# Index weights folded into the key's panel, index scores in two batches between projection units, sums of squares folded by VectorE, and the first conv tap on ScalarE, in a two-layer fp32 kernel

## The chip, the cores and the metric

One Trainium2 chip, one of its cores. The metric is the device time of one execution in microseconds, lower is better. The profile is of one execution; its times are counted from the first instruction (the span's start).

## What is computed

A batch of one, 256 tokens of width 1024, through two layers in fp32. The change touches the first layer's front only:

```
xn = rms_norm(x, norm_g);  z = xn @ w_in          # split: q, c_kv, q_idx, k_idx, w_idx, g_attn, x_rnn, g_rnn, merge
k_idx = layer_norm(k_idx)                         # 64 wide;  c_kv = rms_norm(c_kv), 128 wide
w_idx = w_idx * 8 ** -0.5                         # 8 per token
s_idx[t, s] = sum_j relu(q_idx[t, j] . k_idx[s]) * w_idx[t, j]        # 8 index heads of 64
idx = top_k(causal(s_idx), 64)                    # the keys that attention may look at
out = conv_b + sum_k shift(x_rnn, k) * conv_w[k]  # four taps per channel
r, i = sigmoid(out @ w_a + b_a), sigmoid(out @ w_x + b_x)             # 16 blocks of 64
```

Behind it come attention over the selected keys, the recurrence, gates and output projections, and then a second layer with two attentions and 32 experts. These are the same in both kernels.

## The kernel before

**Layout.** Everything is kept transposed: channels on the 128 partitions, 256 tokens along the free dimension, so x is eight chunks of 128x256. The program is written by hand, one instruction stream per engine, with semaphores.

**Units.** The dense weights come in 140 units of 128x1024 (one output chunk of 128 channels over all eight input chunks). Two units are a panel of 1 MB, and SP loads panels into four slots of `ring`, each when PE has finished with the slot's last panel. A product is made in three passes of rounded operands: ScalarE writes the rounded high part of a unit (L989, `advance`), GpSimd subtracts it from the unit to leave the remainder in place (L1364, two instructions of 128x512 a unit), and TensorE multiplies high by high, high by remainder and remainder by high: 24 matmuls of 256 columns a unit (`chunk`, L450). The high parts have room for four units (`HI_UNITS`), so ScalarE can round unit n only when PE is done with unit n-4, and GpSimd follows ScalarE. PE needs both parts of a unit before its first matmul (`unit`). `PLAN` fixes the order of the units: 0 and 1 are `ckv_kidx`, 2 to 5 `qidx`, 6 to 13 `xrnn`, 14 to 21 `q`. Every two chunks fill one of two PSUM banks D0 and D1, which VectorE or ScalarE releases (`rel`).

**The front.** The first units are multiplied by x times the norm's gain, not yet divided by the root mean square (`x0_hi`, `x0_lo`). Meanwhile ScalarE squares x (L1008), PE sums the squares over the channels by multiplying with a matrix of ones (`sumsq`, L508, plain fp32), ScalarE takes the root (L1015), and VectorE the reciprocal (L1388). VectorE then scales what left D0 (`scaled`), makes the normalised x (`hT`, eight instructions), scales again, and makes the remainder of its rounding (`rest_of`, L1400). From `xrnn` on, units are multiplied by the normalised x. `norm` for the latent and for the index key follow on VectorE, each with a reciprocal.

**Index weights and scores.** w_idx has a small weight of its own, loaded by its own DMA (L372), split by VectorE (L1405, L1400), and multiplied on PE behind the first `xrnn` chunk: 48 matmuls of 8 columns (L543 to L547). The index key is centred by a matmul with a matrix of 1/64 (L535) and a subtraction (L1433). Then the eight heads' scores: two matmuls a head into one of two banks L0 and L1 (L555, L556, plain fp32), relu by ScalarE (L1066), product with the head's weight and sum by VectorE (L1463 to L1470, two instructions a head). A bank is used again when ScalarE has read it, and ScalarE's buffer of two when VectorE has added it. Only then PE goes on with `xrnn` 1 to 7.

**Behind them.** VectorE picks the 64 best by 16 rounds of max and replace (L1476, L1477), makes the mask (L1479, L1480), and then the convolution: four instructions a chunk, each waiting for the one before it (L1485, L1488). PE meanwhile does the eight `q` units, four products for the values (`values`, L574) and the gates' matmuls (`rg_gates`, L567): gates of chunks 0 to 3 behind q 6, of chunks 4 to 7 behind q 7. A gate waits for its chunk's convolution. The attention stage begins with scores (L595) that wait for all gates, and with VectorE instructions that wait for the mask.

## Time and profile before

| | us |
|---|---|
| median of 3 runs (757.46 to 759.19) | 758.28 |
| the profiled execution's own time | 757.45 |
| its span, first to last instruction | 755.7 |
| TensorE busy | 678.2 |
| VectorE busy | 383.3 |
| GpSimd busy | 391.3 |
| ScalarE busy | 331.7 |
| mean granted TensorE clock | 0.973 of full speed |

Busy time is the sum of an engine's instructions. An engine's busy share over the whole span averages stages with different limits; what a stage is worth is read from the order of events in it. A matmul of plain fp32 appears as two records, one of rounded operands as one.

### The profile page before, as it was taken

How to read it: one execution, taken by the hardware profiler on the slowest of the kernel's cores; microseconds unless marked ns; L12 is line 12 of the kernel's file. 1: busy time of each engine (PE TensorE's matmuls, PEld its weight loads, DVE VectorE, ACT ScalarE, POOL GpSimd, SP SyncE). 2: the span in 40 equal slices, each digit the busy share in tenths (PEclk: the TensorE clock that was granted, in tenths of full speed). 3: DMA queues.
4: the chain of work that ended last, by engine and by line, in shares of the span. 5: the costliest groups of instructions: out<-in, count | busy, mean ns of one | idle time of the engine just before them, and what ended most of it. 6: DMA issues, size and time to landing. Idle time of an engine off the chain costs nothing.

```text
span 755.7 us, 13893 instructions
## 1 busy us (share of the span) xinstructions
PE 678.2 (90%) x5634; PEld 564.6 (75%) x5634; DVE 383.3 (51%) x672; ACT 331.7 (44%) x604; POOL 391.3 (52%) x284
## 2 busy tenths in 40 slices
PE   4899999999999999989999999998899998677754
PEld 4879989888998999989789899997745453334321
DVE  3869954489998145996856556433410110010002
ACT  5534476875546346664348755441321211111102
POOL 3837855588878999979879666781000000000000
PEclk9969999999999999999999999999999999999987
DMA  8714533443434455544444334599799999999992
GB/s 326 281 57 141 186 120 112 143 137 112 165 120 163 167 175 200 171 134 160 167 167 168 116 132 144 209 421 423 304 423 419 422 421 421 422 420 422 421 419 88
DMA packets 26274, 181.73 MB, mean 240 GB/s; under 512 B 3040, under 2 KB 3296, under 8 KB 4832
## 3 DMA queue, kind: packets, MB, share of 16 engines
q1 hardware_dynamic: 26208, 180.81, 62.6%
q8 instruction: 47, 0.77, 0.4%
q14 instruction: 19, 0.16, 0.1%
HBM read 179.75 MB, written 1.05 MB: 239 GB/s over the span
## 4 chain that ended last, share of the span: by engine, by line
PE 63%; DMA 13%; DVE 11%; ACT 5%; issue 4%; POOL 2%; SPq 2%; ACTq 0%; DVEq 0%
PE D L450 36%; PE L L869 6%; DMA xT<-w_expert_dram 4%; DMA hT<-w_expert_dram 4%; DMA big<-w_expert_dram 4%; PE L L849 3%; PE QB L899 3%; POOL ring_r L1364 2%; DMA ring<-w_dense_dram 2%; PE D L490 2%; DVE big L1381 2%; PE L L595 1%; PE D L906 1%; DVE big_r L1400 1%; DVE big_r L1405 1%
## 5 line engine op out<-in xcount | busy, mean ns | idle before, releaser
L1364 POOL TENSOR_TENSOR ring_r<-ring,ring_r 128x512 fp32r<-128x512 f32 x280 | 391.1, 1431 | 120.7 <-ACT ring_r L989 120.3
L450 PE MATMUL D<-scr_r,ring_r 128*128 128x256 f32 x1104 | 214.1, 290 | 0.7 <-DVE big L1381 0.7
L989 ACT ACTIVATE ring_r<-ring 128x1024 fp32r<-128x1024 f32 x140 | 146.2, 1053 | 90.9 <-PE D L450 80.4
L450 PEld LDWEIGHTS D<-scr_r,ring_r 128*128 128x128 f32 x1104 | 176.4, 193 | 3.4 <-issue 2.1
L450 PE MATMUL D<-hT_r,ring_r 128*128 128x256 f32 x552 | 156.7, 284 | 0.0
L450 PE MATMUL D<-big_r,ring_r 128*128 128x256 f32 x1110 | 138.1, 284 | 1.6 <-POOL ring_r L1364 1.6
L450 PEld LDWEIGHTS D<-big_r,ring_r 128*128 128x128 f32 x1110 | 134.6, 192 | 3.4 <-issue 2.3
L450 PEld LDWEIGHTS D<-hT_r,ring_r 128*128 128x128 f32 x552 | 106.4, 193 | 1.2 <-issue 1.0
L1381 DVE SCALAR_TENSOR_TENSOR th<-th,L 64x256 f32<-64x256 f32 x32 | 13.4, 418 | 179.7 <-ACT th L1295 179.2
L1295 ACT ACTIVATE th<-L 64x256 f32<-64x256 f32 x16 | 6.0, 377 | 86.1 <-PE L L869 86.1
L849 PEld LDWEIGHTS L<-cst,big 128*128 128x128 f32 x256 | 29.8, 191 | 12.2 <-issue 12.2
L869 PE MATMUL L<-big,small 128*32 128x256 f32 x416 | 29.7, 394 | 8.8 <-DMA big<-w_expert_dram 7.8
L1118 ACT ACTIVATE attn<-attn,stat 128x128 f32<-128x128 f32 x64 | 28.4, 446 | 20.3 <-DVE stat L1508 20.3
L1515 DVE TENSOR_SCALAR attn<-attn,stat 128x128 f32<-128x128 f32 x64 | 34.7, 584 | 1.1
L1400 DVE TENSOR_TENSOR big_r<-big,big_r 128x256 fp32r<-128x256 f32 (+1 forms) x32 | 32.1, 1011 | 6.3 <-ACT big_r L1182 2.8
L849 PE MATMUL L<-cst,big 128*128 128x128 f32 x256 | 32.8, 281 | 1.6 <-DVE cst L1794 0.9
L1285 ACT ACTIVATE small<-L 128x512 f32<-128x512 f32 x16 | 9.6, 597 | 54.3 <-PE L L849 54.3
L869 PE MATMUL L<-ring,small 128*32 128x256 f32 x320 | 23.1, 412 | 10.6 <-DMA ring<-w_expert_dram 10.6
L1126 ACT ACTIVATE attn<-TB 128x384 f32<-128x384 f32 x32 | 15.5, 485 | 34.6 <-PE TB L604 34.6
L869 PEld LDWEIGHTS L<-big,small 128*32 128x32 f32 x416 | 15.9, 112 | 17.9 <-issue 11.4
L869 PEld LDWEIGHTS L<-ring,small 128*32 128x32 f32 x320 | 12.1, 116 | 18.5 <-issue 14.2
L1381 DVE SCALAR_TENSOR_TENSOR big<-big,D 128x512 f32<-128x512 f32 x16 | 10.9, 683 | 27.1 <-PE D L450 27.1
(335 smaller groups left out, 1032.2 us busy)
## 6 DMA issues: line engine op xcount, KB each, us to landing
ring<-w_dense_dram SPq DMA_DIRECT2D x69, 1024.0 KB, 4.9
big<-w_expert_dram SPq DMA_DIRECT2D x40, 1024.0 KB, 25.0
ring<-w_expert_dram SPq DMA_DIRECT2D x30, 1024.0 KB, 26.3
wu<-w_expert_dram SPq DMA_DIRECT2D x6, 1024.0 KB, 24.7
attn<-w_expert_dram SPq DMA_DIRECT2D x5, 1024.0 KB, 20.2
scr<-w_expert_dram SPq DMA_DIRECT2D x5, 1024.0 KB, 27.3
hT<-w_expert_dram SPq DMA_DIRECT2D x5, 1024.0 KB, 27.6
xT<-w_expert_dram SPq DMA_DIRECT2D x5, 1024.0 KB, 26.0
```

The lines of the kernel that those rows point to most:

```text
L450: last = mm(out_, r32(w[i][ws]), r32(x[j][xs_]), start=start and m == 0, stop=stop and m == 2)
L490: mm(bank[:, u * T:(u + 1) * T], r32(w[h][:, k * P:(k + 1) * P]), r32(src[0][:, k, :]), start=(u + k + h == 0), stop=False, skip_group_che ...
L849: last = mm(X[:, c * P:(c + 1) * P], htok[:, tt, (4 * half + c) * P:(4 * half + c + 1) * P], sel[:, g % 2, tt, :], start=(tt == 0), stop=( ...
L869: last = mm(G[at_:at_ + WIN, 0:FF], x(4 * h + k, e), w[e][:, m, k, :], start=(h + k == 0), stop=(h * 4 + k == DC - 1))
L899: last = mm(DN[at_:at_ + WIN, :], actT[:, b, k, e * WIN:(e + 1) * WIN], w[e][:, k, h, :], start=(k == 0), stop=(k == 1))
L989: A_(r32(hi_unit(j)), dense_unit(j), ACT.Copy).then_inc(hi_ready, 1)
L1118: last = A_(E[:, a % 2, c0:c0 + n], S[:, a % 2, c0:c0 + n], ACT.Exp, bias=stat[:, a % 2, 0, tt:tt + 1], accum_out=stat[:, a % 2, 1, tt:tt ...
L1126: A_(PT[:, a % 2, :], TB[:, 0:CAUSAL], ACT.Copy).then_inc(pt_ready, 1)
L1364: last = g.tensor_tensor(r32(w), w, r32(h).bitcast(F32), ALU.subtract)
L1381: return v.scalar_tensor_tensor(out=out_, in0=in0, scalar=scalar, in1=in1, op0=op0, op1=op1)
L1400: v.tensor_tensor(r32(f), f, r32(hi[:, per * i:per * i + per, :]).bitcast(F32), ALU.subtract).then_inc(lo_of[name], 1)
L1515: last = v.tensor_scalar(E[:, a % 2, c0:c0 + n], E[:, a % 2, c0:c0 + n], stat[:, a % 2, 2, tt:tt + 1], None, ALU.mult)
```

## The change

- The eight columns of w_idx take the place of the second copy of the index key in the panel of `ckv_kidx` (64 columns of key, 8 of weights, zeros). The 48 matmuls, their split and their DMA are gone; two matmuls of 8 columns with the identity turn the weights over (L539 of the changed kernel), and ScalarE copies them out.
- The index key is centred by one matmul with a centring matrix of 64 rows, whose result the norm reads from PSUM; the subtraction is gone. The key's norm comes ahead of the latent's.
- The scores go into four banks (L0, L1, TB, OB) in two batches of four heads, one behind `xrnn` 1 and one behind `xrnn` 2. The order of the norm, the units' rounding and the relus on ScalarE is written anew.
- VectorE adds the squares of x pairwise, three additions of 128x512, so that PE sums two chunks, not eight; that sum comes behind `ckv_kidx` 1.
- The convolution's first tap (with the bias) is two ScalarE instructions of 128x256 for each bank of `xrnn`, read from PSUM; VectorE has three instructions a chunk left.
- The softplus of the recurrence's decay and its two table loads come first on ScalarE, and a one-column square root behind unit 1 loads the root's table.
- The values' first matmuls wait for the last relu, since they use two of the four banks.

The diff, cut to its core:

```diff
...
-NORMS = [(8, D), (1, LAT), (1, 1), (8, D), (8, D), (6, QL), (2, KL), (8, D)]
-N_X, N_CKV, N_KIDX, N_FIN1, N_ATT2, N_CQ, N_CKV2, N_FFN = range(8)
+NORMS = [(8, D), (1, IDXD), (1, LAT), (8, D), (8, D), (6, QL), (2, KL), (8, D)]
+N_X, N_KIDX, N_CKV, N_FIN1, N_ATT2, N_CQ, N_CKV2, N_FFN = range(8)
...
+        IB = [L0, L1, TB, OB]
...
-            sp_.dma_start(widx_w[:], w_widx.rearrange("p (c t) -> p c t", c=DC)).then_inc(s_in["widx"], 16)
...
             first_chunk(open_bank("ckv_kidx", 0)[:, 0:T])
-            sumsq(N_X)
             chunk("ckv_kidx", 1, x0)
+            pe.wait_ge(x_folded, 1)
+            for c in range(2):
+                last = mm(UB[:, 0:T], ones, scr[:, c, :], start=(c == 0), stop=(c == 1))
+            last.then_inc(ssq, 1)
             chunk("qidx", 0, x0)
...
-            mm(OB[:, 0:T], C("mean64", P), zc[:, 1, :], start=True, stop=True).then_inc(mean_ready, 1)
+            for tt in range(NT):
+                mm(QB[:, tt * IDXH:(tt + 1) * IDXH], zc[IDXD:P, 1, tt * P:(tt + 1) * P], ident[IDXD:P, IDXD:IDXD + IDXH],
+                   start=(tt == 0), stop=(tt == NT - 1), skip_group_check=True)
+            mm(OB[:, 0:T], C("center", P)[0:IDXD], zc[0:IDXD, 1, :], start=True, stop=True).then_inc(centered, 1)
             chunk("qidx", 1, x0)
-            sumsq(N_CKV, src=sq1)
+            pe.wait_ge(rooted, N_KIDX)
+            pe.wait_ge(sq, SQ0[N_KIDX] + 1)
+            mm(UB[:, 0:T], ones[0:IDXD], sq1[0:IDXD, 1, :], start=True, stop=True).then_inc(ssq, 1)
             chunk("qidx", 2, x0)
-            sumsq(N_KIDX, C("mean64", P), src=sq1[:, 1:2, :])
             chunk("qidx", 3, x0)
+            sumsq(N_CKV, src=sq1)
             chunk("xrnn", 0, h2, split="x")
-            pe.wait_ge(lo_of["widx"], 1)
-            for tt in range(NT):
-                for k in range(DC):
-                    last = mm3(QB[:, tt * IDXH:(tt + 1) * IDXH], h2, (widx_hi, widx_w),
-                               np.s_[:, k, tt * P:(tt + 1) * P], np.s_[:, k, :], k == 0, k == DC - 1)
-            last.then_inc(widx_mm, 1)
+            chunk("xrnn", 1, h2)
+
+            def idx_scores(j0):
+
+                for j in (j0, j0 + 2):
+                    if j >= 4:
+                        pe.wait_ge(idx_relu, j - 2)
+                    for tt, (c0, n) in enumerate(((0, P), (P, T))):
+                        for i in range(2):
+                            lo = IDXD * i
+                            last = mm(IB[(j + i) % 4][:, c0:c0 + n], qi[lo:lo + IDXD, j // 2, tt * P:(tt + 1) * P],
+                                      kiT[lo:lo + IDXD, 0:n], start=True, stop=True)
+                            if tt:
+                                last.then_inc(idx_mm, 1)
...
             pe.wait_ge(kidx_ready, 1)
             kept(pe, "qidx", 1)
...
-            for c in range(1, 8):
+            idx_scores(0)
+            chunk("xrnn", 2, h2)
+            idx_scores(4)
+            for c in range(3, 8):
                 chunk("xrnn", c, h2)
...
+                pe.wait_ge(v1_ready, n - 1) if n >= 2 else pe.wait_ge(idx_relu, IDXH)
...
             squares(N_X, x_in)
+            advance(2)
+            act.wait_ge(vstep, 1)
+            A_(stat[:, 0, 2, 0:1], sp[:, 9, 0:1], ACT.Sqrt)
             advance(HI_UNITS)
             rootmean(N_X)
-            advance(HI_UNITS + 1)
+            advance(HI_UNITS + 2)
+            act.wait_ge(centered, 1)
+            A_(widx, QB[:, 0:2 * IDXH].rearrange("p (a b) -> p a b", a=2), ACT.Copy,
+               scale=float(IDXH ** -0.5)).then_inc(widx_ready, 1)
+            A_(sq1[:, 1, :], OB[:, 0:T], ACT.Square).then_inc(sq, 1)
...
-                   ACT.Copy).then_inc(rel["act"], 1)
-
-            for j in range(IDXH):
-                act.wait_ge(idx_mm, j + 1)
-                if j >= 2:
-                    act.wait_ge(idx_acc, j - 1)
-                A_(S[:, j % 2, :], LB[j % 2][:, 0:CAUSAL], ACT.Relu).then_inc(idx_relu, 1)
+                A_(xr[:, 2 * i:2 * i + 2, CONV:CONV + T], bank[:, :].rearrange("p (a b) -> p a b", a=2), ACT.Copy)
+                for m in range(2):
+                    c = 2 * i + m
+                    last = A_(u[:, c, :], bank[:, m * T:(m + 1) * T], ACT.Identity, bias=V("conv_b", c),
+                              scale=V("conv_w", 3 * 8 + c))
+                last.then_inc(rel["act"], 1)
+
+            def idx_relus(j0):
+
+                for j in range(j0, j0 + 4):
+                    act.wait_ge(idx_mm, j + 1)
+                    if j >= 4:
+                        act.wait_ge(idx_acc, j - 3)
+                    A_(scores_in[:, j % 4, :], IB[j % 4][:, 0:CAUSAL], ACT.Relu).then_inc(idx_relu, 1)
+
+            advance(UNIT0["xrnn"] + 1 + HI_UNITS)
+            idx_relus(0)
             conv_in(0)
+            advance(UNIT0["xrnn"] + 3 + HI_UNITS)
+            idx_relus(4)
...
+            dve.wait_ge(sq, 2)
+            v.tensor_tensor(scr[:, 0:2, :], scr[:, 0:2, :], scr[:, 2:4, :], ALU.add)
+            dve.wait_ge(sq, 4)
+            step(v.tensor_tensor(scr[:, 4:6, :], scr[:, 4:6, :], scr[:, 6:8, :], ALU.add))
+            v.tensor_tensor(scr[:, 0:2, :], scr[:, 0:2, :], scr[:, 4:6, :], ALU.add).then_inc(x_folded, 1)
...
+            dve.wait_ge(centered, 1)
+            norm(N_KIDX, lambda c: OB[:, 0:T], lambda c: kiT, "idx_ln_gain")
+            dve.wait_ge(normed, NM0[N_KIDX] + 1)
+            v.tensor_scalar(kiT, kiT, V("idx_ln_bias"), None, ALU.add).then_inc(kidx_ready, 1)
+            scaled("qidx", 1, qi[:, 2:4, :], float(IDXD ** -0.5))
+            dve.wait_ge(rel["dve"], 1)
+            norm(N_CKV, lambda c: zc[:, 0, :], lambda c: cT, "kv_norm_gain")
...
-                step(v.tensor_scalar(u[:, c, :], xr[:, c, 4:4 + T], V("conv_w", 3 * 8 + c), V("conv_b", c),
-                                     ALU.mult, ALU.add))
...
```

**TensorE, from the first chunk to the third `qidx` unit.** D are the projections' banks, UB holds sums of squares, OB the centred key or its mean, QB the index weights. Before:

```order
L525 MATMUL D<-big_r,ring_r 128x256 x8
L508 MATMUL UB<-scr,vec 128x256 x8
L450 MATMUL D<-big_r,ring_r 128x256 x48
L535 MATMUL OB<-small,cst 128x256
L450 MATMUL D<-big_r,ring_r 128x256 x24
L508 MATMUL UB<-small,vec 128x256
L450 MATMUL D<-big_r,ring_r 128x256 x24
L508 MATMUL UB<-small,cst 128x256
```

and in the changed kernel:

```order
L524 MATMUL D<-big_r,ring_r 128x256 x8
L449 MATMUL D<-big_r,ring_r 128x256 x24
L532 MATMUL UB<-scr,vec 128x256 x2
L449 MATMUL D<-big_r,ring_r 128x256 x24
L539 MATMUL QB<-cst,small 128x8 x2
L541 MATMUL OB<-small,cst 128x256
L449 MATMUL D<-big_r,ring_r 128x256 x24
L545 MATMUL UB<-small,vec 128x256
```

The sum over x moved behind unit 1 and shrank from eight matmuls to two, and the sum behind the first `qidx` pair is now the key's, not the latent's.

**ScalarE, from the rounding of the first units to the key's root.** `scr` is the rounded normalised x, `ring` the units, `root` a root. Before:

```order
L989 ACTIVATE ring_r<-ring 128x1024 x3
L1015 ACT_TABLE_LOAD
L1015 ACTIVATE root<-UB,sp 128x256
L989 ACTIVATE ring_r<-ring 128x1024
L1038 ACTIVATE scr_r<-hT 128x512 x2
L989 ACTIVATE ring_r<-ring 128x1024
L1038 ACTIVATE scr_r<-hT 128x512 x2
L1008 ACTIVATE small<-small 128x256
L1015 ACTIVATE root<-UB,sp 128x256
```

and in the changed kernel:

```order
L1045 ACT_TABLE_LOAD
L1045 ACTIVATE stat<-sp 128x1
L1000 ACTIVATE ring_r<-ring 128x1024 x2
L1026 ACTIVATE root<-UB,sp 128x256
L1000 ACTIVATE ring_r<-ring 128x1024 x2
L1050 ACTIVATE small<-QB 128x16
L1052 ACTIVATE small<-OB 128x256
L1057 ACTIVATE scr_r<-hT 128x512 x2
L1000 ACTIVATE ring_r<-ring 128x1024
L1057 ACTIVATE scr_r<-hT 128x512 x2
L1026 ACTIVATE root<-UB,sp 128x256
```

The table load left the path to the root, the square that PE's next sum needs stands ahead of the rounding of the normalised x and not behind it, and units 4 and 5 are both rounded before it.

**VectorE, from the normalised x to the first addition of scores.** `small` holds the index queries, the key and the latent; D and OB are PSUM. Before:

```order
L1381 SCALAR_TENSOR_TENSOR hT<-xT,vec,th 128x256 x8
L1381 SCALAR_TENSOR_TENSOR small<-D,th 128x512
L1433 TENSOR_TENSOR small<-small,OB 128x256
L1400 TENSOR_TENSOR hT_r<-hT,scr_r 128x512 x4
L1388 RECIPROCAL rinv<-root 128x256
L1381 SCALAR_TENSOR_TENSOR small<-small,vec,rinv 128x256
L1388 RECIPROCAL rinv<-root 128x256
L1381 SCALAR_TENSOR_TENSOR small<-small,vec,rinv 128x256
L1441 TENSOR_SCALAR small<-small,vec 128x256
L1381 SCALAR_TENSOR_TENSOR small<-D,th 128x512
```

and in the changed kernel:

```order
L1401 SCALAR_TENSOR_TENSOR hT<-xT,vec,th 128x256 x8
L1401 SCALAR_TENSOR_TENSOR small<-D,th 128x512
L1420 TENSOR_TENSOR hT_r<-hT,scr_r 128x512 x4
L1408 RECIPROCAL rinv<-root 128x256
L1401 SCALAR_TENSOR_TENSOR small<-OB,vec,rinv 128x256
L1475 TENSOR_SCALAR small<-small,vec 128x256
L1401 SCALAR_TENSOR_TENSOR small<-D,th 128x512
L1408 RECIPROCAL rinv<-root 128x256
L1401 SCALAR_TENSOR_TENSOR small<-small,vec,rinv 128x256
```

The key's reciprocal, product and bias now stand ahead of the latent's, the subtraction is gone, and the key is read from PSUM.

## Rows read from the trace of the kernel before

**Rows 1.** The page: the chain that ended last, by engine.

```profile
PE 63%; DMA 13%; DVE 11%; ACT 5%; issue 4%; POOL 2%; SPq 2%; ACTq 0%; DVEq 0%
```

**Rows 2.** Windows: length, busy us (count) of PE, PEld, DVE, ACT, POOL, clock, DMA.

```profile
42.40:47.70 5.30, 5.30 (x29) 5.28 (x28) 2.57 (x9) 0.21 (x1) 1.19 (x1) 0.52 0.00 0
...
60.00:78.30 18.30, 18.30 (x155) 18.30 (x154) 17.23 (x47) 7.88 (x10) 15.29 (x13) 1.00 0.52 173
```

**Rows 3.** The chain of waits in order of time: start, us, what.

```profile
3.22 0.95 SPq L372
...
20.43 0.49 ACT root L1015
...
20.94 1.77 DVE th L1388
...
30.83 2.87 PE D L450 x24
...
40.11 7.61 PE QB L450 x48
...
56.36 3.73 PE D L450 x17
...
110.90 1.97 PE L L567 x8
```

**Rows 4.** TensorE's timeline: start, us, line, tiles, count, idle before and its releaser.

```profile
15.38 3.62 PE L508 MATMUL UB<-scr,vec 128*128 128x256 f32 x16
...
30.16 0.67 PE L508 MATMUL UB<-small,vec 128*128 128x256 f32 x2 [2.11 <-ACT small L1008]
...
37.07 2.08 PE L473 MATMUL D<-scr_r,ring_r 128*128 128x256 f32 x16
...
116.09 0.93 PE L595 MATMUL L<-small,big 64*128 64x128 f32 x8
```

**Rows 5.** GpSimd's timeline: the remainders of the units.

```profile
14.48 2.50 POOL L1364 TENSOR_TENSOR ring_r<-ring,ring_r 128x512 fp32r<-128x512 f32 x2 [2.29 <-ACT ring_r L989]
18.25 7.73 POOL L1364 TENSOR_TENSOR ring_r<-ring,ring_r 128x512 fp32r<-128x512 f32 x6 [1.28 <-ACT ring_r L989]
28.75 2.97 POOL L1364 TENSOR_TENSOR ring_r<-ring,ring_r 128x512 fp32r<-128x512 f32 x2 [2.77 <-ACT ring_r L989]
```

**Rows 6.** VectorE's timeline, 23 to 56 us.

```profile
23.34 5.30 DVE L1381 SCALAR_TENSOR_TENSOR hT<-xT,vec,th 128x256 f32<-128x256 f32 x8
28.57 0.68 DVE L1381 SCALAR_TENSOR_TENSOR small<-D,th 128x512 f32<-128x512 f32 x1
29.16 0.41 DVE L1433 TENSOR_TENSOR small<-small,OB 128x256 f32<-128x256 f32 x1
29.49 5.08 DVE L1400 TENSOR_TENSOR hT_r<-hT,scr_r 128x512 fp32r<-128x512 f32 x4
34.50 1.74 DVE L1388 RECIPROCAL rinv<-root 128x256 f32<-128x256 f32 x1
36.27 0.99 DVE L1381 SCALAR_TENSOR_TENSOR small<-small,vec,rinv 128x256 f32<-128x256 f32 x1
...
39.99 1.24 DVE L1441 TENSOR_SCALAR small<-small,vec 128x256 f32<-128x256 f32 x1
...
54.32 1.60 DVE L1381 SCALAR_TENSOR_TENSOR small<-attn,small 128x128 f32<-128x128 f32 x4 [0.63 <-ACT attn L1066]
```

**Rows 7.** VectorE's timeline, 58 to 123 us.

```profile
58.17 0.29 DVE L1476 MAX8 small<-small 128x8 f32<-128x128 f32 x1
...
75.22 4.35 DVE L1381 SCALAR_TENSOR_TENSOR big<-big,vec 128x256 f32<-128x256 f32 x3
...
117.12 0.56 DVE L1381 SCALAR_TENSOR_TENSOR attn<-small,L 128x384 f32<-128x384 f32 x1 [11.13 <-PE L L595]
...
121.41 1.67 DVE L1515 TENSOR_SCALAR attn<-attn,stat 128x128 f32<-128x128 f32 x2
```

**Rows 8.** Groups by line and form, VectorE, 0 to 114 us: count, busy us, mean ns.

```profile
L1381 DVE SCALAR_TENSOR_TENSOR big<-big,vec 128x256 f32<-128x256 f32 x24 | 23.8, 992 | 0.9
```

More of the change, by code:

```diff
@@ L113 @@
 _c = 0
-for _name, _n in [("ident", P), ("mean64", P), ("swap", P), ("before", P), ("dist", CAUSAL),
+for _name, _n in [("ident", P), ("center", P), ("swap", P), ("before", P), ("dist", CAUSAL),
                   ("causal", CAUSAL), ("cos_mla", T), ("sin_mla", T), ("cos_moba", T), ("sin_moba", T),
@@ L119, with build @@
 NCST = _c
-def build(nc, x_t, vecs, consts, w_widx, w_rg, w_uk, w_uv, w_kr, w_router, w_dense, w_expert, final_row, out):
+def build(nc, x_t, vecs, consts, w_rg, w_uk, w_uv, w_kr, w_router, w_dense, w_expert, final_row, out):
     ctx = ExitStack()
@@ L206, in build @@
         sq1 = at(small, 2 * K + 512, 2, T)
+        scores_in = at(attn, 0, 4, CAUSAL)
         cqT = at(big, 0, QC, T)
@@ L277, in build @@
         vstep, astep = sem("vector_step"), sem("scalar_step")
-        mean_ready, centered, kidx_ready, widx_mm, widx_ready = [sem(n) for n in (
-            "mean_ready", "centered", "kidx_ready", "widx_matmul", "widx_ready")]
+        x_folded, centered, kidx_ready, widx_ready = [sem(n) for n in (
+            "x_squares_folded", "kidx_centered", "kidx_ready", "widx_ready")]
         idx_mm, idx_relu, idx_acc = sem("idx_scores"), sem("idx_relu"), sem("idx_accumulated")
@@ L1019, in x_in @@
                 return xT[:, c:c + w, :]
-            act.wait_ge(s_in["vec"], 16)
-            act.wait_ge(vstep, 1)
-            A_(root[:, 0:1], sp[:, 9, 0:1], ACT.Copy)
+            act.wait_ge(sp_step, 2)
+            A_(sp[:, 2, :], sp[:, 1, :], ACT.Exp, scale=-1.0).then_inc(sp_act, 1)
+            act.wait_ge(sp_step, 3)
+            A_(sp[:, 4, :], sp[:, 3, :], ACT.Ln).then_inc(sp_act, 1)
             for c in range(DC):
@@ L1408, in _ @@
             step(v.memset(sp[:, 9, :], EPS))
+            dve.wait_ge(s_in["vec"], 16)
+            v.tensor_scalar(sp[:, 0, :], V("lru_lambda", 0, 8), -1.0, None, ALU.mult).then_inc(sp_step, 1)
+            dve.wait_ge(sp_step, 1)
+            v.tensor_tensor(sp[:, 1, :], sp[:, 0, :], V("lru_lambda", 0, 8), ALU.max).then_inc(sp_step, 1)
+            dve.wait_ge(sp_act, 1)
+            v.tensor_scalar(sp[:, 3, :], sp[:, 2, :], 1.0, None, ALU.add).then_inc(sp_step, 1)
+            dve.wait_ge(sp_step, 3)
+            step(v.tensor_scalar(sp[:, 5, :], sp[:, 3, :], 1.0, None, ALU.is_equal))
+            step(stt(sp[:, 6, :], sp[:, 3, :], -1.0, sp[:, 5, :], ALU.add, ALU.add))
+            step(v.reciprocal(sp[:, 7, :], sp[:, 6, :]))
             for c in range(DC):
@@ L1415, in _ @@
             v.memset(xr[:, :, 0:CONV], 0.0).then_inc(padded, 1)
-            v.tensor_scalar(sp[:, 0, :], V("lru_lambda", 0, 8), -1.0, None, ALU.mult).then_inc(sp_step, 1)
-            dve.wait_ge(sp_step, 1)
-            v.tensor_tensor(sp[:, 1, :], sp[:, 0, :], V("lru_lambda", 0, 8), ALU.max).then_inc(sp_step, 1)
-            dve.wait_ge(s_in["widx"], 16)
-            split("widx", widx_w, widx_hi, 0, DC)
+            dve.wait_ge(sp_act, 2)
+            step(v.tensor_tensor(sp[:, 6, :], sp[:, 4, :], sp[:, 5, :], ALU.add))
+            step(v.tensor_tensor(sp[:, 6, :], sp[:, 6, :], sp[:, 2, :], ALU.mult))
+            step(v.tensor_tensor(sp[:, 6, :], sp[:, 6, :], sp[:, 7, :], ALU.mult))
+            step(stt(sp[:, 6, :], sp[:, 0, :], 0.0, sp[:, 6, :], ALU.max, ALU.add))
+            step(v.tensor_scalar(sp[:, 7, :], sp[:, 6, :], LRU_C / 2, None, ALU.mult))
+            v.tensor_scalar(sp[:, 8, :], sp[:, 6, :], -LRU_C / 2, None, ALU.mult).then_inc(sp_ready, 1)
             rinv0 = th[:, 0, 0:T]
@@ L1467, in _ @@
                     acc = score[:, c0:c0 + n]
-                    last = stt(acc, S[:, j % 2, c0:c0 + n], widx[:, tt, j:j + 1],
+                    last = stt(acc, scores_in[:, j % 4, c0:c0 + n], widx[:, tt, j:j + 1],
                                acc if j else C("causal", n, c0), ALU.mult, ALU.add)
@@ L1919, in constants @@
     c["ident"] = np.eye(P)
-    c["mean64"] = ((i[:, None] // 64) == (i[None, :] // 64)) / 64.0
+    c["center"] = np.where(i[:, None] < 64, (i[:, None] == i[None, :] % 64) - 1.0 / 64.0, 0.0)
     r = i % 64
@@ L1960, in pack @@
     uv = k_major(ukv[:, :, HD2:].reshape(KL, 512)).reshape(P, UNIT)
-    parts = [chunks_of(a) for a in (np.concatenate([ckv, ki, ki], 1), qi, xr, q, ga, gr, mg,
+    parts = [chunks_of(a) for a in (np.concatenate([ckv, ki, np.pad(wi, ((0, 0), (0, 64 - IDXH)))], 1), qi, xr, q, ga, gr, mg,
                                     g["w_rnn_proj"][0], g["w_attn_proj"][0], g["w_out"][0], cq, ck, qb, kb)]
```

57 lines of the change are left out of this document (8 added, 49 removed).

## The prediction

> **What bounds the kernel now.** I read the chain of waits by engine first: TensorE holds 63% of it [rows 1], so I look for stretches in which TensorE waits, works slowly or does work that can go. The windows and the chain in order of time show such a stretch in the first layer's front. The 48 matmuls of 8 columns for the index weights take 7.61 us from 40.11 [rows 3], and while they run the granted clock falls: it is 0.52 of full speed from 42.4 to 47.7 [rows 2], so the array is at its lower level, 1.2 GHz of 2.4. The scores behind them last until 56.36, that is 8.64 us, and the next unit still pays for the clock: 17 matmuls in 3.73 us [rows 3], where a unit of 24 takes 2.87 at full clock [rows 3]. Ahead of that TensorE waits once, 2.11 us for a square of ScalarE [rows 4]. From 60 to 78 it has no gap [rows 2], and the gates' last matmuls begin at 110.90 [rows 3]. VectorE is done with the convolution at about 106, since its first attention instruction at 117.12 follows 11.13 us of idleness [rows 7]. So up to the gates TensorE is the path, with some slack for VectorE.
>
> **The sum, followed along TensorE.** I build the times of the changed kernel from the durations of the rows and compare at fixed points.
>
> *To unit 6 (xrnn 0).* Unit 1 starts when its remainder is there, 14.48 + 2.50 = 16.98 [rows 5], and ends at 19.85. The sum over x is now two matmuls; eight took 3.62 [rows 4], 0.45 each, so it ends at 20.75. The squares were there at 15.38 at the latest, when the old sum began [rows 4]; three VectorE additions of 1.27, by the 5.08 for four of that size [rows 6], end by 19.2 and hide behind unit 1. The root takes 0.49, the reciprocal 1.77 [rows 3], the scaling 0.68 [rows 6]: 23.75. The root's table load, which stood just ahead of the root, goes to a place where ScalarE waited for a panel; but the root is no earlier (20.75 against 20.43 [rows 3]), because the sum comes later. Unit 2 has its remainder at 18.25 + 7.73/3 = 20.8 [rows 5] and fills TensorE until 23.7. The transposes and the centring take about 0.7: 24.5. Then unit 3 to 27.3, the key's sum 0.45 to 27.8 (its square is ready, since it now stands ahead of the rounding of x), units 4 and 5 to 33.55, the latent's sum to 34.0. Before, unit 6 began at 37.07 [rows 4]. **Gain 3.1.**
>
> *Index weights.* Gone with their 48 matmuls: **gain 7.6** [rows 3]. Their DMA is 32 KB; its issue, 0.95 on SP and on the chain [rows 3], is gone too, and the panels behind it may land up to that much earlier. I count nothing, since by the path above unit 1 is in place earlier and units 2 and 3 follow closely; the 0.95 goes into the low end.
>
> *Scores.* At full clock a pair of heads of the same shapes takes 0.86 to 0.93, by the attention's own pair [rows 4]. Two batches of two pairs make 3.5, in place of 8.64: **gain 5.1.** The second batch waits for the third relu of the first, which has a whole unit (2.87) to come. What stands behind a late relu on ScalarE is the rounding of units 11 to 13; TensorE comes to those only 8 to 14 us later.
>
> *Clock.* The 17 matmuls at half clock would take 17/24 of 2.87 = 2.03, so **gain 1.7.** Around 30 TensorE was idle for 2.11 and the unit behind it still took 2.87 [rows 3, 4], so I expect the short waits that are left to cost no clock.
>
> *The new wait.* The scores need the key and the second index queries, and these come at the end of a VectorE chain: from 23.75 eight normalised chunks, a scaling 0.68, four remainders 5.08, reciprocal 1.74, key, bias 1.24, scaling 0.68 [rows 6]. The key is read from PSUM now; a product of that size with one operand in PSUM took 0.41, one with both in SBUF 0.99 beside GpSimd [rows 6]. The eight chunks took 5.30 [rows 6], but GpSimd was idle for the last of them, from 25.98 to 28.75 [rows 5], because ScalarE had not rounded unit 5. In the changed order it has, and GpSimd works on. If the last four took 0.40, like small ones alone [rows 6], the first four took 0.92 each; eight of these are 7.4. That makes 41.0. TensorE is through unit 7 at 34.0 + 2 x 2.87 = 39.75. **Loss 1.2**; 0 if the eight take 5.30, 2.5 if key and reciprocals are held up as well.
>
> *Behind it.* ScalarE gets eight taps, 3.9 in all if each takes what the root of the same size took, 0.49 [rows 3], in a stage where it is busy for 7.88 of 18.3 [rows 2]; they are hidden. The five units behind the second batch, q, values and gates are as before.
>
> Sum: 3.1 + 7.6 + 5.1 + 1.7 - 1.2 = 16.3 gained. Against the profiled execution's own 757.45 that is 741.15; the median of the runs is 0.8 higher, so I give **742.0** for the median. Everything behind the gates is started by semaphores and should only move; the loads of the experts too, since the first of them waits for the attentions' last product.
>
> **VectorE, next in line.** The latent follows the key: 41.0 + 1.74 + 0.99 = 43.7, and the additions of scores start there. They took 0.40 each without GpSimd [rows 6]; now GpSimd rounds beside them, and a pair of small instructions beside it took 1.67 [rows 7]. So eight heads take 6.4 to 13.4, ending at 50 to 57. The 16 rounds and the mask took from 58.17 to about 73.8 (75.22 less the first tap, 1.4) [rows 7], 15.6: 66 to 73. The convolution's 24 remaining instructions took 23.8 [rows 8], in a mix of 0.5 alone and 1.45 beside GpSimd [rows 7]: 90 to 97. TensorE asks for the last gates' inputs from 110.9 - 16.3 = 94.6 on, two microseconds long. I count no stall, but the slack of about 5 is nearly spent.
>
> The rows show the additions only with GpSimd idle, so a page bears on them. The Trainium skill (SBUF — State Buffer, "Who interferes with whom") says that a VectorE instruction with two inputs in SBUF contends with GpSimd's reads, and one with at most one such input, outside the two-port modes, does not. That speaks against this change, which moves 16 additions with both inputs in SBUF beside GpSimd's work: by the 0.40 of the rows the forecast stands with its slack, by the rule it moves towards rival 1. The trace agrees with the rule so far, in 0.41 with an operand in PSUM against 0.99 with both in SBUF [rows 6].
>
> **Rivals.**
> 1. *The mask comes late and the convolution stops TensorE* (17%). For it: every addition and tap is slowed beside GpSimd. Against it: GpSimd gets work only as TensorE finishes units, four ahead, so a waiting TensorE soon frees VectorE. Additions 13.4, and all 24 instructions at 1.45, 34.8: 57 + 15.6 + 34.8 = 107.4, against 96: up to 11 lost, 753. A part of it, 3 to 7, is likelier: 745 to 749.
> 2. *The front is quicker* (15%): no new wait, panels 0.95 earlier. 16.3 + 1.2 + 0.95 = 18.5, so 739.8.
> 3. *The gain is given back* (3%): the attention stage or the experts' loads wait for something that did not move, and the time stays at 758. Only the first loads have no semaphore ahead of them, and by the rows above they are used long after.
> 4. *Slower* (3%): VectorE becomes the bound outright. If the 16 additions of scores take 1.45 each (23.2, by the convolution's chained ones [rows 7]), the mask is ready at 82.5 and the convolution at 117.3. The old last gates needed it by about 112, so it decides from 112 on; at 117.3 the kernel loses 5: 763. It needs GpSimd to be busy all the way, which a stopped TensorE prevents.
>
> **How the numbers follow.** The forecast's own case (741 to 744) has 62%, the rivals 17, 15, 3 and 3%. The range 738.8 to 748.0 takes in rival 2 and the likelier part of rival 1. A measurement of this kernel can tell 0.2%, 1.5 us, from no change. Faster 0.95, within it 0.02, slower 0.03.
>
> **What would show it.** In the profile after: unit 6 at about 34 and a granted clock of 1.00 from 37 to 60 (gain of the clock); two batches of scores of under 2 us each, the first after a wait of 0 to 2.5 behind the key; xrnn's last unit ending at about 61.6; VectorE's additions of scores slower than 0.40 each, the first max at 50 to 57; the gates' first matmuls without a wait for the convolution. The forecast is wrong if the clock falls again at the scores, if the first gates wait for VectorE by more than 3, or if the distance from the gates to the end is no longer the same.

## The result, and the profile after

| | before | after |
|---|---|---|
| median of four runs each, us | 758.24 (757.46 to 759.19) | 748.29 (746.90 to 749.74) |
| ratio, with its 95% interval | | 0.9850 (0.9826 to 0.9873) |
| the profiled execution's own time, us | 757.45 | 748.94 |
| its span, us | 755.7 | 747.1 |
| VectorE busy, us | 383.3 | 388.1 |

By the medians the kernel is faster by 10.0 us; the ratio with its interval says 11.4 us (9.6 to 13.2). Forecast were a gain of 16.3 and a time of 742.0, with a range to 748.0; the median lies 0.3 above the range. The page of the changed kernel, its chain by engine:

```profile
PE 56%; DVE 19%; DMA 12%; issue 4%; ACT 4%; POOL 2%; SPq 2%; ACTq 0%; DVEq 0%
```

VectorE has 19% where it had 11 [rows 1]: it has become the path for a stretch. Windows of the changed kernel (columns as in [rows 2]):

```profile
15.50:18.20 2.70, 0.03 (x1) 0.03 (x1) 2.67 (x3) 1.83 (x3) 2.62 (x2) 0.83 1.02 431
18.20:23.60 5.40, 5.40 (x25) 5.40 (x26) 5.15 (x8) 1.29 (x2) 4.98 (x4) 0.50 1.01 419
...
42.40:47.70 5.30, 5.30 (x48) 4.79 (x47) 5.19 (x7) 3.72 (x7) 5.30 (x5) 1.00 0.43 131
```

The clock at the scores is whole now (1.00 from 42.4 on, where it was 0.52), but it is at its lower level from 18.2 to 23.6, where it was 1.00 before. TensorE's timeline:

```profile
18.17 5.49 PE L449 MATMUL D<-big_r,ring_r 128*128 128x256 f32 x24 [2.80 <-POOL ring_r L1384]
23.46 1.36 PE L532 MATMUL UB<-scr,vec 128*128 128x256 f32 x4
...
38.42 2.26 PE L472 MATMUL D<-scr_r,ring_r 128*128 128x256 f32 x16
...
44.45 0.93 PE L560 MATMUL L<-small 64*128 64x128 f32 x8
...
97.90 1.10 PE L579 MATMUL L<-big 128*128 128x256 f32 x4 [0.72 <-ACT big L1099]
100.47 1.13 PE L579 MATMUL L<-big 128*128 128x256 f32 x4 [1.47 <-DVE big L1401]
...
104.83 0.93 PE L606 MATMUL L<-small,big 64*128 64x128 f32 x8
```

Ahead of unit 1 TensorE stands idle for 2.80 us behind GpSimd, and then the unit takes 5.49 us instead of 2.87 [rows 3]. Unit 6 begins at 38.42, later than in the first profile of before (37.07 [rows 4]) and not at 34.0. The wait of 2.11 that stood ahead of the latent's sum [rows 4] is gone. The scores begin without a wait. The last gates, whose second pair began at 110.90 [rows 3], begin it at 97.90, 13.0 earlier, but wait 1.47 in its middle for the convolution. The attention's scores come at 104.83 instead of 116.09 [rows 4]. VectorE's timeline:

```profile
15.23 1.77 DVE L1447 TENSOR_TENSOR scr<-scr 128x512 f32<-128x512 f32 x1
16.92 1.23 DVE L1448 TENSOR_TENSOR both_gains<-vec 128x8 f32<-128x8 f32 x1
...
22.45 1.20 DVE L1458 TENSOR_SCALAR sp<-sp 128x8 f32<-128x8 f32 x1
25.36 1.75 DVE L1408 RECIPROCAL th<-root 128x256 f32<-128x256 f32 x1 [1.71 <-ACT root L1026]
...
27.76 6.24 DVE L1401 SCALAR_TENSOR_TENSOR hT<-xT,vec,th 128x256 f32<-128x256 f32 x8
...
34.52 6.53 DVE L1420 TENSOR_TENSOR hT_r<-hT,scr_r 128x512 fp32r<-128x512 f32 x4
...
42.75 0.48 DVE L1401 SCALAR_TENSOR_TENSOR small<-OB,vec,rinv 128x256 f32<-128x256 f32 x1
43.27 0.35 DVE L1475 TENSOR_SCALAR small<-small,vec 128x256 f32<-128x256 f32 x1
...
47.46 2.80 DVE L1401 SCALAR_TENSOR_TENSOR small<-attn,small,cst 128x128 f32<-128x128 f32 x2
...
79.35 21.07 DVE L1401 SCALAR_TENSOR_TENSOR big<-big,vec 128x256 f32<-128x256 f32 x24
105.86 0.55 DVE L1401 SCALAR_TENSOR_TENSOR attn<-small,L 128x384 f32<-128x384 f32 x1 [5.45 <-PE L L606]
```

The chain of waits of the changed kernel (start, us, what) goes almost wholly by VectorE from the first reciprocal to the last tap:

```profile
27.84 6.16 DVE hT L1401 x8
...
47.46 2.81 DVE small L1401 x2
...
99.05 1.38 DVE big L1401
...
100.47 1.13 PE L L579 x4
```

The additions of scores last from 47.46 to the first max at 62.80, 15.3 us, and 5.45 us of idleness are left where there were 11.13 [rows 7].

**Three distances.** The first matmul comes when x and the first unit have landed, 9.56 to 10.55 us after the start in the thirteen profiles of this study, whatever the kernel. So I cut each profile into: from the first matmul to the start of `xrnn` 0 (*front*); from there to the attention's first scores (*middle*); from there to the end of the span (*rest*).

| profile | front | middle | rest |
|---|---|---|---|
| before | 27.51 | 79.02 | 639.6 |
| before, second profile | 28.62 | 78.99 | 642.0 |
| before with the fold alone | 28.95 | 77.44 | 641.8 |
| after | 28.14 | 66.41 | 642.3 |
| after, second profile | 26.98 | 66.42 | 642.0 |
| no fold | 24.65 | 66.83 | 642.3 |
| filler matmuls | 26.53 | 64.67 | 642.4 |
| fewer rounds | 26.99 | 64.66 | 642.5 |
| mask later | 28.08 | 64.65 | 641.6 |
| no fold and mask later | 25.88 | 64.67 | 642.2 |
| tap back | 26.97 | 69.57 | 641.6 |
| one batch | 26.40 | 68.24 | 644.1 |
| late softplus (filler, mask later) | 25.52 | 64.66 | 640.7 |

Forecast were 24.4 (34.0 less 9.56), 65.8 (79.0 less 7.6, 5.1 and 1.7, plus 1.2) and an unchanged rest. The middle came out within a microsecond, but by luck: the wait for the key that the forecast counted (1.2) did not come, and a wait for the convolution that it did not count (1.8) did. The front did not come out. The rest looks 2.7 us longer than in before's first profile, and not longer than in its second.

### The profile page after: what moved, and what is told of

It reads as the page before. It is cut to its first block, busy times and chain, and to the rows that moved or that the text cites. A ratio compares the mean times of both kernels' runs of the same rounds, so it can differ in the third digit from the quotient of the medians.

```text
span 747.1 us, 13776 instructions
## 1 busy us (share of the span) xinstructions
PE 666.2 (89%) x5578; PEld 554.3 (74%) x5578; DVE 388.1 (52%) x664; ACT 333.6 (45%) x611; POOL 392.8 (53%) x284
## 4 chain that ended last, share of the span: by engine, by line
PE 56%; DVE 19%; DMA 12%; issue 4%; ACT 4%; POOL 2%; SPq 2%; ACTq 0%; DVEq 0%
PE D L449 30%; PE L L880 5%; DVE big L1401 4%; DMA xT<-w_expert_dram 4%; DMA hT<-w_expert_dram 4%; DMA big<-w_expert_dram 4%; PE L L860 3%; PE QB L910 3%; DVE small L1401 2%; POOL ring_r L1384 2%; PE D L489 2%; PE D L917 2%; PE L L606 1%; SPq L388 1%; DVE big_r L1420 1%
## 5 line engine op out<-in xcount | busy, mean ns | idle before, releaser
L449 PE MATMUL D<-big_r,ring_r 128*128 128x256 f32 x1110 | 140.2, 287 | 4.4 <-POOL ring_r L1384 4.3
L449 PEld LDWEIGHTS D<-big_r,ring_r 128*128 128x128 f32 x1110 | 136.7, 195 | 6.7 <-POOL ring_r L1384 3.9
L1401 DVE SCALAR_TENSOR_TENSOR th<-th,L 64x256 f32<-64x256 f32 x32 | 13.4, 418 | 179.4 <-ACT th L1315 178.9
L880 PE MATMUL L<-ring,small 128*32 128x256 f32 x320 | 22.4, 402 | 10.6 <-DMA ring<-w_expert_dram 10.6
## 6 DMA issues: line engine op xcount, KB each, us to landing
xT<-w_expert_dram SPq DMA_DIRECT2D x5, 1024.0 KB, 27.6
```

The source lines that it names most:

```text
L449: last = mm(out_, r32(w[i][ws]), r32(x[j][xs_]), start=start and m == 0, stop=stop and m == 2)
L880: last = mm(G[at_:at_ + WIN, 0:FF], x(4 * h + k, e), w[e][:, m, k, :], start=(h + k == 0), stop=(h * 4 + k == DC - 1))
L1401: return v.scalar_tensor_tensor(out=out_, in0=in0, scalar=scalar, in1=in1, op0=op0, op1=op1)
```

## The experiments

Ratios are to the kernel before, run on the same chip. All but the second profile of before were timed in five rounds. By their ratios alone the first four variants of the changed kernel (no fold, filler, fewer rounds, mask later) cannot be told from it, since their intervals overlap its 0.9805 to 0.9857; their readings rest on the distances above.

**The changed kernel again**, without an edit.

> The changed kernel once more, as the base for the others. Expected 748.3 in the median, with a wider spread than the kernel before (746.9 to 749.7 in four runs). If the granted clock at short gaps is a matter of the moment, its profile may show the half clock in other places than the first one did (unit 1 at 18 us, the qb units at 320, the router at 515).

Measured: 747.19 us (745.16 to 748.35) against 760.19 for before, ratio 0.9831 (0.9805 to 0.9857). This is the line that the next three compare with.

**No fold.** VectorE's three additions go, and eight chunks are summed ahead of unit 1:

```
-            chunk("ckv_kidx", 1, x0)
-            pe.wait_ge(x_folded, 1)
-            for c in range(2):
-                last = mm(UB[:, 0:T], ones, scr[:, c, :], start=(c == 0), stop=(c == 1))
-            last.then_inc(ssq, 1)
+            sumsq(N_X)
+            chunk("ckv_kidx", 1, x0)
```

> Undoes the folding of x's squares alone: no VectorE additions, eight sums ahead of unit 1. Theory A (the fold leaves TensorE idle for 2.8 us ahead of unit 1, and the clock halves for unit 1, 5.49 in place of 2.87): TensorE is busy through the gap, unit 1 takes 2.87, the root comes at 21 in place of 24.85, all of VectorE's chain moves with it, 744 to 745. Rival B (the gap costs nothing that the eight sums, 2.7 longer on TensorE, do not cost as well): 748, no change.

Measured: 745.12 us (743.2 to 746.52), ratio 0.9801 (0.9775 to 0.9828). TensorE's timeline of this kernel:

```profile
15.05 3.61 PE L507 MATMUL UB<-scr,vec 128*128 128x256 f32 x16
18.32 6.10 PE L449 MATMUL D<-big_r,ring_r 128*128 128x256 f32 x48
...
34.77 2.26 PE L472 MATMUL D<-scr_r,ring_r 128*128 128x256 f32 x16
```

The sums fill what was the gap, unit 1 and 2 together take 6.10, and the front is 24.65, 2.3 less than in the changed kernel's second profile and 3.5 less than in its first. It is also 2.9 less than before's 27.51. The other kernel without the fold (further down) has 25.88, so one profile can be off by a microsecond. On the mean of two profiles each, the front was 28.1 before, 27.6 in the changed kernel and 25.3 without the fold: the new order of the rest of the front is worth some 2.8 us, and the fold takes 2.3 of them back. A part goes elsewhere: the first reciprocal begins at 19.74 and not at 23.89 as in the changed kernel's second profile, but GpSimd is then busy all through the normalised x, which takes 10.6 us instead of the 6.24 of the changed kernel's first profile (VectorE's groups from 20 to 36 us):

```profile
L1398 DVE SCALAR_TENSOR_TENSOR hT<-xT,vec,th 128x256 f32<-128x256 f32 x8 | 10.6, 1388 | 0.0
```

**Filler.** The fold stays, and twenty matmuls whose product nobody reads stand in the gap:

```
+            for n in range(20):
+                mm(QB[:, 0:T], r32(x0_hi[:, 0, 0:P]), r32(x0_hi[:, 1, :]), start=True, stop=True)
             chunk("ckv_kidx", 1, x0)
```

> The changed kernel with 20 matmuls of 256 columns, result unused, in the gap ahead of unit 1. Only the clock is changed: unit 1 starts at 18.2 as now. Theory A: unit 1 takes 2.87, the sums 0.9, the root comes 2.8 earlier; 745.5. Rival C (unit 1 was slow because of late operands, or the clock falls all the same): unit 1 still takes 5.5 and the time stays at 748.3.

Measured: 745.28 us (745.14 to 745.64), ratio 0.9811 (0.9788 to 0.9833).

```profile
15.02 2.55 PE L530 MATMUL QB<-big_r 128*128 128x256 f32 x20
17.62 3.14 PE L449 MATMUL D<-big_r,ring_r 128*128 128x256 f32 x24
```

Unit 1 takes 3.14 again, and the granted clock from 17.6 to 20.6 was 1.00. Nothing but idle time of TensorE was filled, so the 2.35 us that unit 1 took longer in the changed kernel's first profile (1.5 in its second, which has 4.63) are the clock, and they are lost because the eight sums no longer stand there. The sum is ready at 21.3 and the root at 22.1, but the reciprocal begins only at 23.17: VectorE still has small instructions of 1.2 us each beside GpSimd. So the front gains only 0.5 to 1.6.

**Fewer rounds.** The key choice is cut from eight rounds to six a tile, so it keeps 48 keys and not 64: `for r in range(TOPK // 8 - 2)`.

> Leaves out two of the eight rounds of max and replace for each half of the tokens (48 keys are kept, not 64), so VectorE has 3.3 us less between the scores and the convolution. If VectorE binds only at the last gates, where TensorE waited about 1.6 us in the changed kernel, the gain is 1.6 and the rest becomes slack: 746.7. If VectorE were the bound throughout, 3.3: 745. If it binds nowhere: 748.3.

Measured: 745.9 us (743.79 to 745.97), ratio 0.9804 (0.9778 to 0.9829). With the same front as the changed kernel's second profile (26.99 and 26.98) the middle is 1.76 shorter, though VectorE has 3.3 less to do. That is the wait for the convolution (1.48 in that profile, and some 0.3 because it breaks the gates' last eight matmuls in two: 1.10 and 1.13 for 1.97) and no more.

**Fold alone**, put into the kernel before (three additions on VectorE, two sums behind unit 1).

> The kernel before with one part of the change put in alone: VectorE adds x's squares together, and TensorE sums two products behind unit 1 instead of eight ahead of it. Theory A (the sums ahead of unit 1 were the work that kept TensorE's granted clock up while GpSimd finished unit 1's rest): TensorE is idle 2 to 3 us ahead of unit 1, the clock falls to its lower level, the first square root's input comes at about 24 instead of 20.4, and the kernel is slower than before by 1 to 4 us (ratio 1.001 to 1.005). Theory B (the fold is worth what the prediction gave it): faster by about 3 us, ratio 0.996. Theory C (unit 6 is held by the roundings and not by the square root): no difference within 1 us.

Measured: 761.9 us (758.68 to 763.93, 12 runs) against 760.31 (757.02 to 761.82, 17 runs), ratio 1.0021 (1.0005 to 1.0037): slower by 0.4 to 2.8 us. That the fold is worth about 3 us (theory B) is ruled out, and so is any gain from it in this kernel. Theory B asked too much of it, though: of the prediction's 3.1 only 0.9 was the fold's (the second unit's end at 23.7, where the trace of before has the centring at 24.59), and 2.1 was the wait ahead of the latent's sum, which the new order of ScalarE was to remove. The gap and the clock are there without any other part of the change:

```profile
17.81 4.64 PE L451 MATMUL D<-big_r,ring_r 128*128 128x256 f32 x24 [2.32 <-POOL ring_r L1368]
```

The front is 28.95, longer than in both profiles of before. The middle is 1.6 shorter than theirs, because the clock at the index weights and scores stayed low for less time: its mean over the 24 us from unit 6 was 0.72, where it was 0.64 in both profiles of before, which is 1.9 us of full clock. Together the two distances are no longer than before; where the 1.6 us of the median lie this one profile does not show.

**Mask later.** Four of the sixteen rounds and the two mask instructions move behind the convolution on VectorE; nothing is left out:

```
-                for r in range(TOPK // 8):
+                for r in range(TOPK // 8 - (4 if tt else 0)):
...
-            step(v.tensor_scalar(score, score, TAKEN / 2, -BIG, ALU.is_gt, ALU.mult))
-            v.tensor_tensor(Dm, score, C("dist", CAUSAL), ALU.add).then_inc(mask_ready, 1)
...
                 ins.then_inc(conv_done, 1)
+            s = score[:, P:P + T]
+            for r in range(4):
+                step(v.max(out=top8[:, 1, :], in_=s))
+                step(v.match_replace(out=s, in_to_replace=top8[:, 1, :], in_values=s, imm_value=TAKEN))
+            step(v.tensor_scalar(score, score, TAKEN / 2, -BIG, ALU.is_gt, ALU.mult))
+            v.tensor_tensor(Dm, score, C("dist", CAUSAL), ALU.add).then_inc(mask_ready, 1)
```

> The changed kernel with four of the sixteen rounds of the key choice and the two instructions that turn it into the mask moved behind the convolution on VectorE; nothing is left out. Theory A (the last gates' matmuls wait for the convolution, by 1.6 to 1.8 us, and VectorE has over 5 us free ahead of the first attention head): the convolution ends about 5.5 us earlier, the wait goes, the attention starts 1.6 to 1.8 us earlier, and the time is 745.5 beside 747.2 for the unchanged kernel on the last chip (ratio to before 0.981). Theory B (the wait for the convolution is only where another wait is seen, the values' or the ScalarE chain's): no difference, 0.983. Theory C: the mask, now ready last, holds the first attention head: slower than the changed kernel by 0.5 to 2 us.

Measured: 745.74 us (743.24 to 747.14), ratio 0.9799 (0.9776 to 0.9821). TensorE and VectorE of this kernel:

```profile
97.31 1.96 PE L579 MATMUL L<-big 128*128 128x256 f32 x8 [0.72 <-ACT big L1099]
```

```profile
97.88 1.50 DVE L1515 TENSOR_TENSOR small<-small,cst 128x384 f32<-128x384 f32 x1
103.53 0.55 DVE L1401 SCALAR_TENSOR_TENSOR attn<-small,L 128x384 f32<-128x384 f32 x1 [4.14 <-PE L L606]
```

The wait is gone, the middle is 64.65 instead of 66.41, and the mask is ready 4 us before it is wanted. The same work in another order is worth 1.76, the price of the wait.

**No fold and mask later**, both edits.

> The changed kernel with the fold undone (eight sums of squares ahead of unit 1, as before) and the mask's end moved behind the convolution on VectorE. Theory A (two losses that add: 2.1 us for the fold, 1.7 us for VectorE ahead of the last gates, more than the 1.7 since without the fold VectorE had become the later one): 743 us or a little under, ratio 0.977 to 0.978. Theory B (the same 2 us counted twice): 745, ratio 0.980.

Measured: 744.44 us (743.03 to 744.92), ratio 0.9787 (0.9770 to 0.9804). Front 25.88 and middle 64.67: both gains are there at once. The interval of the times holds theory A's 0.977 to 0.978 and also theory B's 0.980, and the times cannot separate this kernel from either edit alone (745.1 and 745.7); the distances speak for theory A.

**Before again**, for a second profile.

> The kernel before, unchanged, for a second profile. If the granted clock falls to its lower level behind the gap of 2.3 us ahead of the second pair of the query projection (about 331 us) and at the router (about 525 us) in this profile too, then what the changed kernel seems to give back there is a difference between executions, and not of the kernels. If both stay at the full level, as in the first profile of before while four profiles of the changed kernel and its variants showed them fallen, the change gives back about 2.5 us there.

Measured: span 760.2 and an own time of 762.09. It has the lower clock at the router (0.60 and 0.55 in the two windows from 526 to 530), as every profile but the first of before has, and it keeps the full clock at 331. Its rest is 642.0. So the 2.7 us that seemed given back behind the attention are a difference between two executions of the kernel before. TensorE's timeline of this profile shows one more thing, to be read beside the wait of 2.11 of [rows 4] and the 2.87 of a unit [rows 3]:

```profile
30.99 0.74 PE L508 MATMUL UB<-small,vec 128*128 128x256 f32 x2 [2.82 <-ACT small L1008]
31.31 4.72 PE L450 MATMUL D<-big_r,ring_r 128*128 128x256 f32 x24
```

Here the wait was 2.82, and the unit behind it took 4.72.

**Tap back.** The convolution's first tap goes back to VectorE (32 instructions), and ScalarE's two a bank go.

> The changed kernel with the convolution's first tap back on VectorE (32 instructions instead of 24) and the three ScalarE instructions at a projection bank back to one. Theory A (VectorE sets the last gates, and now has 8 instructions of 0.4 to 0.9 us more ahead of them, while the convolution's wait is already 1.5 to 1.8 us): 4 to 7 us later at the last gates, all of it on the path, so 751 to 754 where the changed kernel has 747.2 to 748.3 (ratio to before 0.988 to 0.992). Theory B (the change's VectorE slack of some 5 us at the attention would have carried the tap): under 1.5 us slower, ratio at most 0.985.

Measured: 750.83 us (749.75 to 752.45), ratio 0.9891 (0.9874 to 0.9907). The tap on ScalarE is worth about 0.006, 4.6 us, by the ratios; the medians differ by 3.6, and the middle by 3.2. TensorE waits for the convolution twice, and the clock falls behind it (four matmuls of the same kind took 1.13 in the changed kernel):

```profile
99.17 1.65 PE L579 MATMUL L<-big 128*128 128x256 f32 x4 [3.48 <-DVE big L1397]
101.06 2.08 PE L579 MATMUL L<-big 128*128 128x256 f32 x4 [0.24 <-DVE big L1397]
```

**One batch.** Both batches of scores stand right behind `xrnn` 1:

```
             idx_scores(0)
-            chunk("xrnn", 2, h2)
             idx_scores(4)
+            chunk("xrnn", 2, h2)
```

> The changed kernel with both batches of index scores right behind the second projection chunk, as one, instead of one projection chunk between them. Theory A (the chunk between covers ScalarE's four rectifications and VectorE's additions, of 2.8 us for the first pair): TensorE waits 2 to 4 us between the batches, then the clock falls for some us, and it is slower by 2 to 4 us than the changed kernel (ratio 0.987 to 0.989). Theory B (VectorE is what sets the gates, and a wait on TensorE here costs nothing behind it): no difference, ratio 0.983 to 0.985.

Measured: 745.94 us (745.38 to 750.28), ratio 0.9819 (0.9804 to 0.9834): no difference, theory B. I had expected TensorE to wait 2 to 4 us between the batches. The profile is of the slowest execution, 750.28; the other five lie between 745.38 and 746.72.

```profile
44.03 0.93 PE L560 MATMUL L<-small 64*128 64x128 f32 x8 [0.30 <-ACT attn L1080]
...
98.58 2.08 PE L579 MATMUL L<-big 128*128 128x256 f32 x4 [1.60 <-DVE big L1401]
```

The wait between the batches is 0.30: the third relu is done 0.3 us after the second batch asks for its bank. So the unit between the batches buys nothing that can be measured; four banks and a ready key make the scores short. In this profile the wait for the convolution was 1.60, and the four matmuls behind it took 2.08 and not 1.13, which is most of why its middle is longer. Ahead of unit 1 the gap was 1.85 here, shorter than in the six other profiles of kernels with the fold and no filler (2.23 to 2.80), and this time the clock did not fall:

```profile
17.63 3.14 PE L449 MATMUL D<-big_r,ring_r 128*128 128x256 f32 x24 [1.85 <-POOL ring_r L1384]
```

**Late softplus.** Fold, filler and mask later, and in addition the product of two gains and the last six small instructions of the softplus (L1448, L1452 to L1458) move from ahead of the first reciprocal to behind the convolution.

> The changed kernel with three edits: twenty matmuls whose product is never read keep TensorE busy in the gap ahead of unit 1 (the fold is kept), the mask's end stands behind the convolution, and the last seven small instructions on the gate's decay with the product of two gains stand there too, instead of ahead of the first reciprocal on VectorE. Theory A (in the run with the twenty matmuls alone the reciprocal came at 23.17 although the sum was there at 21.3, since VectorE still had the small instructions beside GpSimd): the reciprocal at about 21.5, unit 6 about 1.5 us earlier than in that run, no wait for the convolution, and the time at 742 to 743.5 (ratio 0.976 to 0.978). Theory B (GpSimd's subtractions beside the normalised x take the gain back, as in the run without the fold): 744.5, ratio 0.979.

Measured: 744.11 us (742.55 to 744.36), ratio 0.9794 (0.9779 to 0.9808). The reciprocal waits for the root now, and begins at 22.35 instead of 23.17:

```profile
22.35 1.75 DVE L1410 RECIPROCAL th<-root 128x256 f32<-128x256 f32 x1 [4.40 <-ACT root L1028]
```

The front is 25.52, 1.0 less than with the filler alone; I had expected 1.5. By the times it cannot be told from the kernel without fold and with the later mask. Both beat the changed kernel (0.9831 and 0.9850): the five runs of this one (742.55 to 744.36) lie below all five that the changed kernel had on the same chip (745.16 to 748.35), and the interval of the other one (0.9770 to 0.9804) lies wholly below the changed kernel's (0.9805 to 0.9857).

## Why the prediction was right and wrong, by its own steps

*To unit 6 (xrnn 0)*: **this step failed.** Forecast was a gain of 3.1 and a start at 34.0; it was 38.42, a loss of 1.35 against before's first profile. By the fronts of all four profiles it was between a loss of 0.6 and a gain of 1.6. The part of the step that removed the wait of 2.11 held; the part that counted on the fold did not. Of the 4.4 us between 34.0 and 38.42, 1.2 come from unit 1 starting at 18.17 and not 16.98 (x landed later in this execution, and GpSimd's remainder took 2.93, not 2.50), 2.4 from its length to the next matmul, 5.29 and not 2.87, 0.1 from the sum and 0.7 from what lies between the sum and unit 6. The 2.4 are what the step overlooked. It placed unit 1 at 16.98, while unit 0 ends at 15.4 [rows 4], and so it had a gap of 1.6 us where TensorE was busy before; I reasoned only about when the sum would be ready, and let the gap cost nothing. The eight sums were also a filler, work that kept TensorE busy while it waited for GpSimd. The runs with no fold, with filler and with the fold alone show that.

*Clock*, its last sentence, "I expect the short waits that are left to cost no clock": wrong. I had taken it from one wait of 2.11 with a fast unit behind it. Here 2.80, 2.32 and 2.23 brought the lower level, though 1.85 did not, and in the second profile of before 2.82 did at the very wait that had been 2.11. The other part of the step, 1.7 for the scores, held: 1.00 from 42.4 to 47.7.

*Index weights*, *Scores*: right as a sum. Unit 6 to the last gates took 13.0 + 1.35 = 14.35 us less; the three gains of 7.6, 5.1 and 1.7 make 14.4. This is the greater part of the whole gain, and it rests on the traces of the two kernels: no run undoes these parts one by one. *The new wait*: mis-sized, 0 and not 1.2, and not for a reason that the step gave. The key with its bias was there at 43.6 and the second index queries at 44.2 (forecast for both: 41.0), since the normalised x began 4.0 later (27.76, forecast 23.75); but TensorE was through unit 7 only at 44.45 (forecast 39.75). The eight chunks took 6.24 and not 7.4, the four remainders 6.53 and not 5.08; the bias took 0.35 and not 1.24.

*VectorE, next in line*: the additions of scores took 15.3 and not 6.4 to 13.4. By size (groups of VectorE from 45 to 66 us of the changed kernel; before, both sizes together took 0.40 on the mean [rows 6]):

```profile
L1401 DVE SCALAR_TENSOR_TENSOR small<-attn,small 128x256 f32<-128x256 f32 x7 | 6.4, 920 | 0.0
L1401 DVE SCALAR_TENSOR_TENSOR small<-attn,small 128x128 f32<-128x128 f32 x7 | 5.9, 841 | 0.7
```

The means hide two prices. GpSimd's timeline has a pause of 3.00 us in the middle of the additions, and the chain of waits gives their times in pairs, one small and one large:

```profile
37.08 17.06 POOL L1384 TENSOR_TENSOR ring_r<-ring,ring_r 128x512 fp32r<-128x512 f32 x12
57.14 13.07 POOL L1384 TENSOR_TENSOR ring_r<-ring,ring_r 128x512 fp32r<-128x512 f32 x10 [3.00 <-ACT ring_r L1000]
```

```profile
50.37 2.62 DVE small L1401 x2
...
55.63 0.76 DVE small L1401 x2
...
56.48 0.76 DVE small L1401 x2
...
57.34 2.70 DVE small L1401 x2
```

In the pause (54.14 to 57.14) a pair took 0.76 of the chain, as cheap as in the kernel before; while GpSimd was subtracting, a pair took 2.6 to 2.8. So of the 16 additions the seven that began in the pause cost their old price, 0.35 or 0.48 each, and the nine others 1.18 to 1.51. Beside GpSimd the forecast's price for a pair, 1.67, was too low.

The convolution, 21.1 for 24 instructions, was no longer than its price of 23.8 [rows 8]. It ended at 100.4, behind my 90 to 97, and TensorE waited 1.47 for it: **"I count no stall" was wrong by 1.76**, the difference that fewer rounds and the later mask took away. That is a small form of rival 1, which had 17%. The rule of the Trainium skill (SBUF — State Buffer, "Who interferes with whom"), that two inputs in SBUF contend with GpSimd's reads, bears on this: the trace agrees, with 1.18 to 1.51 for such additions beside GpSimd and 0.48 for the key's product, which also ran beside it but has one of its inputs in PSUM.

*Behind it*: right, the taps cost nothing on ScalarE. Their value was not in the sum at all, since there was no stall to remove; the run with the tap back puts 3.2 to 4.6 us on it. By the ratios (0.9891 and 0.9831) the change without the tap would have been worth some 8 us where it is worth 13 with it.

Sum at the attention's start: 16.3 less 4.4 for the front, plus 1.2 for the wait that was not there, less 1.8 for the convolution, is 11.3; the trace has 116.09 - 104.83 = 11.26. The medians gave 10.0 in the first runs and 13.0 in the second; the rest of the program differs from one execution to the next by more than what is left to explain.

Of rival 2 only the missing wait came, not the quicker front. Rival 3 did not happen, and rival 4 neither: GpSimd is not busy all the way. None of the prediction's three signs of being wrong came (the clock at the scores, a wait of the gates over 3, another distance from the gates to the end): all three looked behind unit 6, and the step that failed lies ahead of it.

## What to carry to other kernels

Before an instruction is taken off an engine, ask whether it was only filling a wait for something else; then what it saves is idle time, and TensorE's idle time can cost its clock on top. Write the gaps that your own placed times leave into the sum, with a price each. When work moves beside an engine that slows it, here VectorE's additions beside GpSimd, price all of it at the slowed rate before counting on slack; and look for instructions that nobody wants for some time yet (the mask, the softplus) and put them behind the ones that somebody waits for.
